# Making the fourth layer's modulation with TensorE products of weight blocks and a vector, in place of weighted sums on DVE

## What is computed

```python
def second_block(x, c, positions, w_ada, b_ada, norm_g, w_in, conv_w, conv_b, ...):
    c_act = jax.nn.silu(c)
    for l in range(DEPTH):                                   # DEPTH = 2
        ada = c_act @ w_ada[l] + b_ada[l]                    # (1, 1024) @ (1024, 3072)
        shift, scale, gate = jnp.split(ada, 3, axis=-1)
        h = rmsnorm(x, norm_g[l]) * (1.0 + scale[:, None, :]) + shift[:, None, :]
        p = h @ w_in[l]
        ...                                                  # heads: mLSTM 0 to 3, retention 0 to 3
        x = x + gate[:, None, :] * (y @ w_out[l])
    return rmsnorm(x, final_g)
```

## Time and profile before

| | |
|---|---|
| median of 3 runs | 3738.32 us |
| the profiled execution, its own time | 3736.55 us |
| its span in the profile | 3734.7 us |
| mean granted clock of TensorE | 0.942 |
| PE / weight loads / DVE / ACT / POOL busy | 93% / 62% / 40% / 21% / 39% |
| chain of work that ended last | PE 84%, DVE 9%, POOL 3%, ACT 2% |
| third layer, first product to the first L988 | 2292.58 to 2930.60 us of the span |
| fourth layer, the same | 3019.42 to 3629.99 us |

### The profile page before, as it was taken

One profiled execution on the slowest core, in us unless ns is written; L12 is line 12 of the kernel. 1 busy time (PEld: TensorE's weight loads), 2 busy tenths in 40 slices (PEclk: granted clock), 3 DMA queues, 4 the chain that ended last, 5 costly groups with the idle time before them and its releaser, 6 DMA issues.

```text
span 3734.7 us, 37648 instructions
## 1 busy us (share of the span) xinstructions
PE 3459.2 (93%) x13991; PEld 2316.4 (62%) x13991; DVE 1482.7 (40%) x2529; ACT 782.3 (21%) x1349; POOL 1442.5 (39%) x1372
## 2 busy tenths in 40 slices
PE   6999978999999999987899998999999989999998
PEld 5665554666666556443554444887897458889953
DVE  5121438753344231235753224355554233344321
ACT  2211313222111031222221111223211013321110
POOL 0008989900000000899100002767563047776600
PEclk6999987999999999978899998999999999999999
DMA  5111000002232111111004331222222222222211
GB/s 185 45 34 34 29 23 23 1 12 89 92 94 89 52 51 45 40 34 34 1 18 124 124 100 57 75 95 91 91 94 87 58 68 68 68 68 69 79 43 47
DMA packets 259174, 236.41 MB, mean 63 GB/s; under 512 B 20870, under 2 KB 257202, under 8 KB 258996
## 3 DMA queue, kind: packets, MB, share of 16 engines
q1 hardware_dynamic: 258996, 234.02, 20.5%
HBM read 231.90 MB, written 2.10 MB: 63 GB/s over the span
## 4 chain that ended last, share of the span: by engine, by line
PE 84%; DVE 9%; POOL 3%; ACT 2%; issue 1%; DMA 0%; DVEq 0%; ACTq 0%; SPq 0%; POOLq 0%
PE ps L396 34%; PE ps L880 20%; PE ps L426 10%; PE ps L634 3%; PE ps L660 3%; DVE arena L1397 3%; DVE arena L1401 2%; PE ps L930 2%; DVE arena L1403 2%; PE ps L646 2%; PE ps L574 2%; ACT arena L1025 1%; PE ps L412 1%; PE ps L974 1%; PE ps L504 1%
## 5 line engine op out<-in xcount | busy, mean ns | idle before, releaser
L396 PE MATMUL ps<-hT,wring 128*128 128x512 f32 (+1 forms) x1568 | 577.5, 528 | 2.5 <-ACT arena L1025 2.5
L396 PE MATMUL ps<-arena,wring 128*128 128x512 f32 (+1 forms) x1280 | 493.5, 544 | 10.6 <-DVE arena L1397 10.6
L396 PEld LDWEIGHTS ps<-hT,wring 128*128 128x128 f32 x1568 | 301.1, 193 | 266.5 <-issue 248.1
L1921 POOL TENSOR_TENSOR arena<-wring 128x512 f32<-128x512 f32 x72 | 93.5, 1298 | 950.4 <-DMA wring<-in_w_in 642.7
L1885 POOL TENSOR_TENSOR arena<-arena,posi 128x512 f32<-128x512 f32 (+1 forms) x360 | 413.5, 1149 | 30.0
L426 PE MATMUL ps<-hT,wring 128*128 128x512 f32 (+1 forms) x1088 | 417.0, 537 | 0.0
L396 PEld LDWEIGHTS ps<-arena,wring 128*128 128x128 f32 x1280 | 243.3, 192 | 247.6 <-issue 228.2
L1397 DVE TENSOR_TENSOR arena<-arena 128x768 f32<-128x768 f32 (+7 forms) x141 | 185.6, 1316 | 382.1 <-ACT arena L1025 378.6
L426 PEld LDWEIGHTS ps<-hT,wring 128*128 128x128 f32 x1088 | 206.0, 194 | 183.2 <-issue 174.0
L1025 ACT ACT_TABLE_LOAD x148 | 189.9, 1283 | 509.7 <-PE ps L504 113.3
L1025 ACT ACTIVATE arena<-ps 128x256 f32<-128x256 f32 (+6 forms) x307 | 135.8, 442 | 695.5 <-PE ps L396 305.7
(11 more groups left out here) (175 smaller groups left out, 4710.0 us busy)
## 6 DMA issues: line engine op xcount, KB each, us to landing
wring<-in_w_in SPq DMA_DIRECT2D x128, 1024.0 KB, 5.3
wring<-in_w_mod SPq DMA_DIRECT2D x24, 1024.0 KB, 7.9
wring<-in_w_out SPq DMA_DIRECT2D x24, 1024.0 KB, 5.5
wring<-in_w_ada SPq DMA_DIRECT2D x24, 1024.0 KB, 5.1
wring<-in_w_conv_out SPq DMA_DIRECT2D x8, 512.0 KB, 3.5
wring<-in_w_gla_out SPq DMA_DIRECT2D x8, 512.0 KB, 4.0
wring<-in_w_attn_out SPq DMA_DIRECT2D x8, 512.0 KB, 4.0
arena<-in_x SPq DMA_DIRECT2D x1, 2048.0 KB, 9.8
```

The source lines that it names most:

```text
L396: last = eng.matmul(o_(out), a, b_, start=(i == 0), stop=(i == len(parts) - 1))
L1921: pool.link(eng.tensor_tensor(t1, w[:, 0:4, P:2 * P], w[:, 0:4, 0:P], ALU.subtract))
```

## The change

For the fourth layer the steps "mod load" are gone, from PE's program and from DVE's; at the steps "mod", in their old places, PE loads the group through `weights` and multiplies it by the direct way. ACT's part is as before. What the other layers do is as before.

```diff
@@ steps2, proj
             mods = []
             if i == 0 and 2 <= n < 8:
                 mods = [("mod", n, 2 * n - 3)]
-            elif i == 2 and 1 <= n < 7:
-                mods = [("mod load", n, 2 * n - 2)]
             elif i == 3 and 1 <= n < 7:
-                mods = [("mod", n, 2 * n - 2), ("mod load", n, 2 * n - 1)]
+                mods = [("mod", n, 2 * n - 2)]
             yield [("corners", n, i)] + mods
@@ PE's program
-                    if kind == "mod load":
+                    if kind == "mod":
                         if l < DEPTH - 1:
-                            mod_load(L + 1, x[0])
-                    elif kind == "mod":
-                        if l < DEPTH - 1:
-                            mod_finish(L + 1, x[0])
+                            modulate(L + 1, [x[0]])
                     elif kind == "out":
@@ DVE's program
                 for kind, n, *x in steps2():
                     h, r, b = n % 4, n // 4, n % 2
-                    if kind == "mod load":
-                        if l < DEPTH - 1:
-                            dve.stage("modulation")
-                            modulate(L + 1, x[0])
-                            dve.stage("cell")
-                    elif kind == "products":
+                    if kind == "products":
                         i = x[0]
```

## The result

The changed kernel takes 3765.14 us (median of four runs, 3764.38 to 3772.61), against 3741.23 us for the kernel before in the same comparison; the ratio is 1.0066 (95% interval 1.0046 to 1.0086), about 25 us slower. The forecast was 36 us slower, 3774.6 us in a range of 3747 to 3791 us. One execution of the kernel before (10170.84 us) and one of an experiment (12684.01 us) stand far outside all others and are left out of the ratios.

The account below looks back on a forecast made before the run. PE's work, waits and clock were taken to bound the kernel. -27.45 + 43.0 - 4.9 + 25.7 = +36.3 us on the profiled 3736.55 us gave 3772.9 us, and 1.8 us to the median made 3774.6 us; range 3747 to 3791 us.

Parts of the forecast that it names:

- the count of 10: Third layer: 10 of the 12 added runs expected to lower PE's clock, at 2.57 us each, +25.7 us.
- DVE's sums and their waits removed: Third layer: 96 DVE instructions, 48 small matmuls and the waits they bring go, -27.45 us, the difference to the fourth layer.
- 384 weight-load-paced matmuls: Third layer: 32 added one-column matmuls per group, 0.112 us each set by the weight load, +43.0 us.
- waits covered at the transpositions: Odd groups' runs stand in three 1.64 us PE waits on DVE before transpositions (L979), -4.9 us.
- ACT's reading: PE's three waits for ACT's reading of the modulation (L958) could stay, 0 to +3.3 us; taken as 0.
- loads and pair sums: Weight loads keep number and size but change ring places; they and GpSimd's pair sums were expected covered, 0 us.
- clock: Third layer: PE's clock falls behind most of the 12 one-column runs, +25.7 us, bounds nothing to 73 us.
- The base: The fourth layer, 610.57 us without modulation, taken as the third layer's state without it (638.02 us before).
- Rival 2: Second weight load of each product hides under the first, 0.056 us each, clock held: -10.9 us, 3727 us; chance 0.04.
- Rival 1: The clock holds through the third layer's added runs: +10.6 us, 3749 us; chance 0.12.
- Rival 3: Clock falls early in most runs or stays low until the next: clock term 41 to 73 us, 3790 to 3822 us; chance 0.08.
- Rival 4: PE's product waits come from DVE's other work and stay in part: some 3782 to 3789 us; chance 0.04.

Follow-up runs that it names:

- second profile: The changed kernel run and profiled again, nothing altered: median 3773.03 us, ratio 1.0084 to the kernel before, third-layer stretch 667.42 us.
- 128-column kernel: Changed kernel with each product's vector column streamed 128 times instead of once: ratio 1.0021 to the kernel before, 8 us slower, stretch 648.40 us.
- two of the experiments: Changed kernel with 128 streamed columns (ratio 1.0021 to before), and with each group's two blocks made at two steps, 24 runs of 16 matmuls (ratio 1.0025).
- doubled kernel: Changed kernel with each of a group's 16 products made twice, 64 one-column matmuls a run instead of 32: ratio 1.0287 to before, 107 us slower.

## Why the prediction was right

The sign, the mechanism and the place hold; the time is inside the range, the forecast 5 to 11 us too high by the two ratios. That the clock falls behind most runs, and not all, was a judgement from four rows; the count of 10 had no working of its own, and it is what was off. By its steps, for the third layer:

| term | predicted | measured |
|---|---|---|
| DVE's sums and their waits removed | -27.45 | product waits 20.2 to 5.7 us; fourth layer 610.48 |
| 384 weight-load-paced matmuls | +43.0 | 12 x 3.49 = +41.9 |
| waits covered at the transpositions | -4.9 | 10.9 - 6.0 = -4.9 |
| ACT's reading | 0 | 0 |
| loads and pair sums | 0 | 0, no wait of PE on DMA or GpSimd |
| clock | +25.7 | +18.1, +19.8 in the second profile |
| sum | +36.3 | +27.55; +29.4 |

*The base.* Taking the fourth layer as the state without modulation was the step that carried most, and the one that the 128-column kernel tests: 610.5 + 12 x 3.57 - 5.0 = 648.3 us, measured 648.40.

*The price of a load.* 0.109 us measured, 0.112 taken from products of 128 columns. With 128 columns it is indeed 3.57 / 32 = 0.112. The Trainium skill's figure for few columns ("TensorE: Matmul & The Clock Gate", section "Back-to-back issue gap"), which spoke for the change, leaves the weight load out by its own words; matmuls that each need their own load take 0.109 us here and can't be priced by it. Rival 2, a second load that vanishes, is refuted by the same number.

*The clock.* This term was mis-sized. It is what remains of the stretch, 665.57 - 610.48 - 41.9 + 4.9 = 18.1 us, and the 128-column kernel gives the same from the other side (665.57 - 648.40 + 42.8 - 41.9 = 18.1). I had counted 10 falls at 2.57 us. The price of each can be read: from the first matmul of a run to the start of the third group of eight behind it, a run that fell takes longer than a like one that didn't, by 1.7 us (five times) or 3.3 us (three times), 18.4 us in all. In the second profile it is four times 1.7 and three times 3.3 us, 16.7 us; the rest of its 19.8 us lies elsewhere, mostly at the stretch's ends (its first 16 matmuls took 9.71 us against 8.71 in the first profile, its last 35 us had a mean clock of 0.90 against 1.00). So the two prices that the prediction took the mean of, 1.73 and 3.4 us, both occur, with a mean of 2.3 to 2.4 us, and the number of falls was too high: I took all runs to be closer to the waits that had lowered the clock, and let two off, while four and five got through. The bounds (7 to 12 falls) hold both. One of the rows was misread on the way: what stands before the wait of 2.89 us is not "4-column work" but two matmuls of four partitions and 512 columns,

```profile
2373.36 1.10 PE L945 MATMUL ps<-arena,const 4*128 4x512 f32 x2
```

so it says little of what few columns do; no term was taken from it. Rival 1, the clock holds, is what two of the experiments make true by design, and they land where it said, 8 and 9 us slower than before against its 10.6. The rule of the Trainium skill ("TensorE: Matmul & The Clock Gate", section "Why this matters for your kernels"), that steady work keeps the clock up, would have given that time for the change itself; PE was busy 644 of 666 us, in the second run 4.31 of 4.31 us, and the clock fell all the same. Rival 3 shows only in the doubled kernel. Rival 4 is refuted by PE's waits.

*Faster than before?* Not with all 12 groups on PE in this form and these places: without any fall the runs cost 42 us, and what they remove or cover is worth 32 us. The three groups that stop PE are worth moving, by either way.

What stays open: why the sums of 3.61 us and of 8.73 us differ. In the kernel before their length goes with GpSimd's work in all 12 groups: six take 3.61 us and GpSimd is busy 0.00 us of it, three take 6.4 us with 3.9 us of GpSimd, three take 8.8 us with 8.3 us. One of each (length, PE, its loads, DVE, ACT, GpSimd, clock, DMA):

```profile
2425.64:2429.25 3.61, 3.61 (x18) 3.18 (x17) 3.39 (x7) 0.64 (x2) 0.00 (x0) 1.00 0.84 280
2692.01:2698.40 6.39, 5.88 (x29) 5.24 (x30) 6.18 (x7) 1.45 (x5) 3.87 (x3) 1.00 0.45 150
2440.92:2449.71 8.79, 5.25 (x25) 4.28 (x23) 8.58 (x7) 2.91 (x5) 8.30 (x7) 0.99 0.21 75
```

That is a strong sign, not a proof: no kernel here takes GpSimd's work away and leaves the rest, and the share of DMA differs too. Nor was it tried why the kernels that move or halve the sums of groups 1, 3 and 5 stay 12 to 16 us above the 616 us that the parts would allow; the waits shown are most of it. What decides whether a given run of the changed kernel falls is open as well; its place doesn't.

## What to carry to other kernels

Before moving vector-matrix work to TensorE, price it by its weight loads, since here a column cost as much as 128, and subtract only the waits that the old way really puts on the bound engine: here three of 12 groups made the long product waits. Where such products must stand in a row, stream more columns or break the run up between full products; here the one cost 0.08 us a run and the other nothing to be seen, and both kept the clock. If the same layer runs elsewhere without the part in question, its length is a good base for the sum: for the kernel with 128 columns it gave the stretch to within 0.1 us.

## What the runs showed of the hardware

- 32 matmuls of one f32 column take 3.49 us and of 128 columns 3.57 us at full clock, weight load included. Streaming 128 times as much is all but free, and it makes the third layer 17 us shorter than one column does.
- Of 12 like runs of 3.49 us, eight brought a fall of the clock in one execution and seven, partly others, in the next; of 24 runs of 1.70 us between full products, none did. A fall cost 1.7 or 3.3 us, 2.3 to 2.4 us on average.
- The same seven weighted sums on DVE took 3.61 us and 8.73 us in one execution; in the kernel before, 3.61 us with GpSimd idle and 8.8 us with GpSimd busy 8.3 us of it.
